# A hybrid attention, state-space and PEER layer: head-by-head decoding, a second buffer for turned tiles, and moved table steps and row copies

## What is computed

```python
h = layer_norm(x)                                   # 512 x 2048
z = h @ w_in                                        # q, k, v, ssm_in and two gates
y_attn = chunk_attention(q, k, v); y_ssm = s5(u)    # 8 heads; 64 groups
y_ssm = y_ssm * sigmoid(y_ssm @ w_ssm_glu)
merged = sigmoid(g_attn) * (y_attn @ w_attn_up) + sigmoid(g_ssm) * (y_ssm @ w_ssm_up)
h = layer_norm(alpha * h + merged @ w_mix_out)
ple = rms_norm(p @ ple_w_in) * sigmoid(h @ ple_w_gate)
# PEER: 8 heads pick 16 of 128 x 128 experts for each token
sc = (h @ w_q) . sub_keys                           # 8 x 2 x 128 scores
cand = top16(sc[0]) + top16(sc[1]);  top_sc, pos = top16(cand)     # pos -> pair of indices
gates = softmax(top_sc)
act = gelu(h . u_table[expert]);  y = sum((gates * act) * v_table[expert])
out = layer_norm(alpha * h + y + ple)
```

## Time and profile before

| | |
|---|---|
| median of 3 runs | 3962.52 us (3962.35 to 3972.41) |
| the profiled execution | 3965.28 us, its span 3963.5 us |
| busy | PE 3700.7 us (93%), DVE 2861.7 (72%), POOL 2312.2 (58%), ACT 1140.4 (29%) |
| mean granted clock of PE | 0.974 of full speed |
| memory traffic | 1020.65 MB read, 344.45 MB written |

### The profile page before, as it was taken

How to read it: one execution, slowest core, us unless ns; L and a number is a source line. 1 busy time by engine, 2 the same in 40 slices (tenths; PEclk the granted TensorE clock), 3 DMA queues, 4 the chain that set the end, 5 groups by cost and what they waited for, 6 DMA issues and landing times. The chain is left out here.

```text
span 3963.5 us, 49639 instructions
## 1 busy us (share of the span) xinstructions
PE 3700.7 (93%) x17969; PEld 3211.3 (81%) x17969; DVE 2861.7 (72%) x3863; ACT 1140.4 (29%) x1377; POOL 2312.2 (58%) x1290
## 2 busy tenths in 40 slices
PE   6999999999988999999999999999918999999998
PEld 5778888787767688879999999999817888888886
DVE  7666666667762445869778656666658999999998
ACT  3232322333211332223333222222202333333332
POOL 7334343344433234446666648888877888887870
PEclk9999999999999999999999999999959999999999
DMA  6888888887877586998998889999878999999994
GB/s 230 279 292 279 291 284 283 288 294 275 296 260 255 185 296 226 387 397 279 351 313 276 276 286 341 339 342 339 330 282 345 388 373 382 383 382 373 386 374 188
DMA packets 409612, 1231.15 MB, mean 311 GB/s; under 512 B 77561, under 2 KB 122633, under 8 KB 327977
## 3 DMA queue, kind: packets, MB, share of 16 engines
q1 hardware_dynamic: 261784, 770.07, 55.9%
q0 software_dynamic: 63488, 302.31, 20.2%
q10 hardware_dynamic: 84240, 157.63, 10.8%
HBM read 1020.65 MB, written 344.45 MB: 344 GB/s over the span
## 5 line engine op out<-in xcount | busy, mean ns | idle before, releaser
L767 POOL TENSOR_TENSOR wlo<-raw,whi 128x1024 fp32r<-128x1024 f32 x296 | 758.8, 2586 | 1075.2 <-ACT whi L1122 527.7
L1315 PE MATMUL bank<-h_hi,whi 128*128 128x384 f32 (+1 forms) x3312 | 1191.9, 360 | 41.6 <-DVE wlo L1642 37.2
L1317 PE MATMUL bank<-h_hi,wlo 128*128 128x384 f32 (+1 forms) x3312 | 1181.3, 357 | 0.0
L1316 PE MATMUL bank<-h_lo,whi 128*128 128x384 f32 (+1 forms) x3312 | 1180.5, 356 | 0.0
L1315 PEld LDWEIGHTS bank<-h_hi,whi 128*128 128x128 f32 x3312 | 625.4, 189 | 99.9 <-DVE wlo L1642 45.4
L1317 PEld LDWEIGHTS bank<-h_hi,wlo 128*128 128x128 f32 x3312 | 624.9, 189 | 50.2
L1316 PEld LDWEIGHTS bank<-h_lo,whi 128*128 128x128 f32 x3312 | 625.6, 189 | 47.9 <-issue 0.2
L1642 DVE TENSOR_TENSOR wlo<-raw,whi 128x2048 fp32r<-128x2048 f32 x240 | 549.3, 2289 | 142.0 <-ACT whi L1241 84.6
L1613 PE MATMUL bank<-whi,ew_hi 128*128 128x512 f32 x1408 | 550.1, 391 | 98.1 <-DVE ew_lo L1642 95.9
L834 POOL DMA_INDIRECT gates_d<-gate_all,place_u x336 | 496.0, 1476 | 148.3 <-issue 129.8
L1615 PE MATMUL bank<-whi,ew_lo 128*128 128x512 f32 x1408 | 548.8, 390 | 0.0
(11 more groups left out here) (302 smaller groups left out, 4713.4 us busy)
## 6 DMA issues: line engine op xcount, KB each, us to landing
raw<-in_weights SPq DMA_DIRECT2D x388, 1024.0 KB
v_rows_d<-in_weights ACTq DMA_DIRECT2D x96, 1024.0 KB
tin<-in_weights SPq DMA_DIRECT2D x162, 512.0 KB, 6.0
u_rows_d<-tout SPq DMA_DIRECT2D x324, 256.0 KB, 6.8
u_rows_d<-u_tout SPq DMA_DIRECT2D x188, 256.0 KB
v_rows_d<-in_weights SPq DMA_DIRECT2D x32, 1024.0 KB
gates_d<-zeros SPq DMA_DIRECT2D x32, 768.0 KB, 16.1
act_d<-act_o ACTq DMA_DIRECT2D x128, 192.0 KB
```

Source lines behind the costliest of these rows:

```text
L767: pool.tensor_tensor(wlo[slot][:, part], raw[slot][:, part], whi[slot][:, part].bitcast(F32), ALU.subtract).then_inc(lo_made, 1)
L1315: pe.matmul(bank, whi[slot][:, cols], rhs_hi(c), start=c == 0, stop=False)
L1316: pe.matmul(bank, whi[slot][:, cols], rhs_lo(c), start=False, stop=False)
L1317: last = pe.matmul(bank, wlo[slot][:, cols], rhs_hi(c), start=False, stop=c == DC - 1)
```

## The change

- `tout` becomes two buffers with a semaphore each. In the heads all steps use the first; from the up stage on they alternate. `u_tout` lies elsewhere, and DVE's up loop is written out.
- `OUT_STEPS` 9, three ahead of each column group; units 4 to 53 are turned in the U stage, 50 of them. In the output stage SP issues `ln_g`, `ln_b` and the ple weights behind slab 12's load and ahead of slab 13's.
- POOL makes the low parts of units 0 and 1 only (`U_POOL` 2), DVE those from 2 on.
- The decoding is cut into four pieces for each of 8 heads, which stand behind the low parts of units 2 to 46 (`decode_slab`); scatters of a head can begin when its `place` is done. `sum_gates` follows `sums_by`.
- Row copies: 24 in the gating stage, one behind each of units 0 to 3, then two in four units up to unit 67.
- Five `u_row` buffers. The dots stand behind units 56 to 122. SP loads V's first weights behind the load of unit 122; DVE makes them behind the low parts of units 124 to 127. The gelu of the dots moves behind ACT's second V slab.

```diff
-U_POOL = 16
+U_POOL, U_TURN = 2, 4
...
-UP_STEPS, OUT_STEPS = 16, 12
+UP_STEPS, OUT_STEPS = 16, 9
...
-U_ROWS = 3
-U_LAYS = SB - HEADS - N_GLU // 2 - (N_Q // 2 - 1) - N_GATE // 2
+U_ROWS = 5
+GATE_LAYS_AT = HEADS + N_GLU // 2 + N_Q // 2 - 1
+U_LAYS_AT = GATE_LAYS_AT + 6
+AUX_FROM = N_U - 6
...
-    return 67 + 4 * k // 7
+    first = TURN_U.stop + 2
+    return first + k * (N_U - 5 - first) // PICKS
+def decode_slab(u):
+    return 2 + u if u < 4 else 6 + (u - 4) * 3 // 2
...
-    tout = sb("tout", [P, 4, DC, 32], c_at + 8 * kb)
+    tout = [sb(f"tout{k}", [P, 4, DC, 32], c_at + at * kb) for k, at in enumerate((8, 24))]
...
+            load_wide(AT_OUT, N_OUT - 4)
+            for k in range(2):
+                sp.wait_ge(tout_stored[k], 64 * TOUTS[k] + 64 * (1 - k))
+            sp.dma_start(ln_g[:, :], row(2)).then_inc(ln1_landed, 16)
+            sp.dma_start(ln_b[:, :], row(3)).then_inc(ln1_landed, 16)
             sp.wait_ge(h_ready, TT)
             sp.dma_start(pw_sb[:, :, :], ple_w).then_inc(ple_landed, 16)
             sp.dma_start(p_sb[:, :, :], p_t).then_inc(ple_landed, 16)
-            for i in range(N_OUT - 4, N_OUT):
+            for i in range(N_OUT - 3, N_OUT):
                 load_wide(AT_OUT, i)
...
+                if e == AUX_FROM:
+                    for t in range(TD):
+                        sp.wait_ge(gate_placed[t], 16 * PICKS)
+                    for h in range(2):
+                        sp.wait_ge(act_stored[h], 16 * 8 + 16)
+                    for q in range(4):
+                        load_aux(0, q)
...
-                dve.wait_ge(tout_stored, 64 * x + 64)
+                if k == 0:
+                    dve.wait_ge(tout_stored[0], 64 * (x if used is None else used) + 64)
+                elif used > 0:
+                    dve.wait_ge(tout_stored[1], 64 * used)
...
-            dve.wait_ge(h_tok_landed, 64)
-            dots, sums = 0, TOPK
+            dots, sums, decoded = 0, TOPK, 0
             for e in range(U_POOL, N_U):
                 if e in TURN_U:
                     turn_unit(e)
                 low_part_of(e - U_POOL, e % 2, raw[e % 2])
-                while sums < min(PICKS, TOPK + 3 * (e - U_POOL + 1)):
+                while decoded < 4 * RH and decode_slab(decoded) <= e:
+                    decode(decoded)
+                    decoded += 1
+                    if decoded == 4 * RH:
+                        tables()
+                while sums < sums_by(e):
                     sum_gates(sums)
                     sums += 1
                 while dots < PICKS and dot_slab(dots) <= e:
...
+                if e >= N_U - 4:
+                    first_weights(e - N_U + 4)
```

More of the change, by code:

```diff
@@ L317, in build_trunk @@
     h_tok = sb("h_tok", [P, D], a_at + 56 * kb)
-    u_row = [w(f"u_row{i}", [P, D], at) for i, at in enumerate((24, 56, 64))]
+    u_row = ([w(f"u_row{i}", [P, D], at) for i, at in enumerate((24, 56, 64))]
+             + [sb(f"u_row{3 + i}", [P, D], c_at + 8 * i * kb) for i in range(2)])
     act_p = w("act_p", [P, PICKS], 75.5)
@@ L1927, in _ @@
                     dve.drain()
-            with dve.Fori(0, DC // 2) as j:
+            for j in range(DC // 2):
                 for s in range(2):
@@ L1958, in _ @@
             for g in range(3):
-                for n in range(4):
-                    turn_slab(HEAD_STEPS + UP_STEPS + 4 * g + n)
+                for n in range(3):
+                    x = HEAD_STEPS + UP_STEPS + 3 * g + n
+                    turn_slab(x, *turned_in(x))
                 dve.wait_ge(blk_done, BLK_OUT + 4 * g + 4)
@@ L2083, in _, with picked @@
             dve.sem_inc(picks_made, 1)
-            dve.tensor_scalar(pos_a[:, :, :], pos[:, :, :], 4, None, ALU.logical_shift_right)
-            dve.tensor_scalar(pos_b[:, :, :], pos[:, :, :], 15, None, ALU.bitwise_and)
-            dve.drain()
-            dve.tensor_copy(pos_af[:, :, :], pos_a[:, :, :])
-            dve.tensor_copy(pos_bf[:, :, :], pos_b[:, :, :])
-            dve.drain()
-            with dve.Fori(0, RH) as j:
-                at, one, two = bass.ds(j * TOPK, TOPK), bass.ds(2 * j, 1), bass.ds(2 * j + 1, 1)
-                wide = [P, TT, TOPK, TOPK]
-                for t in range(TT):
-                    for eq, of in ((eq_a, pos_af), (eq_b, pos_bf)):
-                        tt(eq[:, t, :, :], iota[:, 0:TOPK].unsqueeze(1).to_broadcast([P, TOPK, TOPK]),
-                           of[:, t, at].unsqueeze(2).to_broadcast([P, TOPK, TOPK]), ALU.is_equal)
+            def picked(j):
+                return slice(j * TOPK, (j + 1) * TOPK)
@@ L2098, in _, with keep_index, choose @@
+            def keep_index(j):
                 dve.drain()
-                for eq, half in ((eq_a, one), (eq_b, two)):
-                    tt(eq[:, :, :, :], eq[:, :, :, :], i_all[:, :, half, :].to_broadcast(wide), ALU.mult)
+                for eq, half in ((eq_a, 2 * j), (eq_b, 2 * j + 1)):
+                    tt(eq[:, :, :, :], eq[:, :, :, :], i_all[:, :, half:half + 1, :].to_broadcast(wide), ALU.mult)
+            def choose(j):
                 dve.drain()
                 for eq, sel in ((eq_a, sel_i), (eq_b, sel_j)):
-                    dve.tensor_reduce(sel[:, :, at], eq[:, :, :, :], AX.X, ALU.add)
@@ L2139, in weighted, with decode @@
+            def decode(u):
+                if u % 4 == 0:
+                    compare(u // 4)
+                elif u % 4 == 1:
+                    keep_index(u // 4)
+                elif u % 4 == 2:
+                    choose(u // 4)
+                else:
+                    place(u // 4)
             def weighted(q):
```

217 lines of the change are left out of this document (118 added, 99 removed).

## The result

The change makes the kernel faster, by less than half of what was forecast: 3923.6 us (median of 4 runs, 3920.1 to 3924.3) against 3964.6 (4 runs) for the kernel before; the ratio is 0.9891, 95% interval 0.9875 to 0.9906. That is 41 us less where the prediction says 93 (3869), and it lies just inside the upper end of the range, 3925.

A forecast was written before the change was run, and what follows sets the result against it. Bounds: DVE's store waits in the early stages, then POOL's row of 312 slow indirect DMAs in U. 18 + 18 + 6 + 52 + 2 - 3 = 93 us off gave 3869 us for the median (own range 3835 to 3905, wide 3790 to 3925).

The forecast's parts named there:

- The direction and the place of what bounds: U stage, units 56 to 122: POOL's 312 gathers and scatters hold DVE's dots and so PE; faster, chance 0.92.
- Up stage: Two tout buffers end DVE's wait for the store ahead of up_a: 18 of 22 us won.
- Output stage: Two buffers, nine steps and reordered loads let PE set the pace, the opening gaps staying: 18 of 41 us won.
- Gating stage: Eight of 32 row copies go and PE sets the pace: 6 of 7 us won.
- It fits, nearly ... I let the low part of unit 53 come 446 us after the stage's start.: U stage, units 0 to 55: DVE's load is at most 8.1 us per unit where PE needs 8.32.
- Rival (b): Front of U stays bound by stores: units 4 to 53 at 9.25 us, not 8.4; 42 us, 3911; chance 0.13.
- I take 2.10 ... 665 in all.: U stage: POOL's 312 operations at 2.10 us each, 665 us from first gather to the last dot's end.
- From the last dot to V: End of U: a low part, 2 us, and five units, 42; last dot at 1123, V at about 1169.
- The clock's ramp and the third V slab: Start of V: 2 us won as the clock's ramp after the gap goes, 3 lost loading the third V slab.
- Rival (a): POOL keeps up; DMA traffic bounds units 56 to 122, 570 us for 67 units; about 3780; chance 0.17.
- Rival (c): Up and output stages held by tin and loads, not the store, and POOL takes 2.25 us: 3958; chance 0.04.
- Rival (d): Slower: decode pieces in DVE's queue make units 4 to 46 take 11.3 us each; 125 us, 3994; chance 0.06.

The follow-up runs named there:

- turns_first: h_in_psum with DVE turning the output stage's first two slabs before it adds b_ln_in to res, not after: 3794.4 us.
- three_stores: h_in_psum with h_tok loaded after the last turned unit's store and a third buffer for turned units in the U stage: 3792.2 us.
- dot_one_input: The changed kernel with each dot replaced by a sum of the gathered row alone, one SBUF input (wrong output): 3807.5 us.
- h_in_psum: The changed kernel with h_tok copied once into four idle PSUM banks, where each dot reads its second input: 3812.3 us.
- both: h_in_psum with the edits of turns_first and three_stores together, nothing left out: 3781.0 us.

## Where the prediction held and where it failed

**The direction and the place of what bounds.** Right. PE was held by DVE, DVE by the gathered rows, and those by POOL; with 184 operations fewer the time fell by 112 us. The gap before V went, and PE's loss spread over units 56 to 122, as the text said. The saving was mis-sized all the same: 41 us for 93, because the U stage gave nothing where 52 were forecast. The result is 19 us out of the forecast's own range, 3835 to 3905; in the wide one it lies by 1 us.

**Up stage.** Right and a little low: 23 us gained for 18. DVE does wait for `tin`, 4.8 us in all, but it doesn't reach PE, which is busy all of 174.20 us.

**Output stage.** 14 us for 18. That the opening stays was foreseen, but it was left in the sum as an unavoidable piece. `turns_first` shows that it was an order of two operations in DVE's queue, worth 18 us.

**Gating stage.** 8 us for 6.

**"It fits, nearly ... I let the low part of unit 53 come 446 us after the stage's start."** This is the step that failed first: unit 53 came at +466, 21 us late, with 3 more for a last store that took 16 instead of 12 us. I added up DVE's operations against PE's 8.3 us, and that sum was right (`three_stores` runs at PE's pace with all of them). But a sum of busy times leaves out the loop: transpose, store, free buffer. It goes round once in two units, and the store had become late in busier queues. The row that told it was at hand, 3.59 us of waiting in a kernel with one piece of work less. Rival (b), given 0.13, had the mechanism, with 9.25 us per unit for the 8.8 that were measured: 24 of its 42 us. With the next two misses, 22 and 7 us, and 4 us more than forecast from the early stages, that makes 3918 of the measured 3924.

**"I take 2.10 ... 665 in all."** The second step that failed. The mechanism was right and the size off: 2.15 us per operation, and 687 us from the first gather to the end of the last dot, so 22 us more. The 2.07 of the earlier trace rows comes from the middle of the row; over all of it, less POOL's waits for a buffer, it was 2.04 before. What made it 2.15 no run shows. The "less a little" at the end didn't come, and the way from the last gather to the last dot was taken from the wrong gather (16.8 us instead of 10.6); that it measures 19.3 in after, so that the error did little harm, is luck. The sum took the pace from DVE's busy share ("the busier DVE, the slower POOL"). What counts is DVE's operations with two SBUF inputs, which the prediction names only further down; beside a transpose or a sum of one input there is no stretch. In `dot_one_input` DVE was busier (84%) and POOL faster (1.77 us), so the mix, not the busy share, should have been carried over.

**From the last dot to V:** 53 us for 46, and the prediction's own terms give 44 (1123 + 2 + 42 = 1167, not 1169). The next low part waited 7.6 us for `whi`, and ACT for its slab, while the first weights of V were being loaded.

**The clock's ramp and the third V slab,** 2 us won and 3 lost. V takes 981.5 us to the end of the program, against 979.6. The ramp is gone: before, the first twelve V matmuls start 0.43 us apart, at a granted clock of 0.51, and in after 0.23 from the first on, at 1.00: 2.5 us less. PE's waits for V's low parts rise from 2.1 to 6.2 us instead. Both terms were of the right size.

**Rival (a), POOL keeps up.** It did not, but its price can be read now. With `h_tok` in PSUM the row takes 555 us from the first to the last gather and 578 to the end of the last dot, against the 570 that (a) gave for its 67 units. PE is busy 544.57 of the 555 us and DMA's share is 1.00, at 395 GB/s, so both are full and the runs don't tell which would hold alone. "DMA: Bandwidth & Descriptors" of the Trainium skill, section "Bandwidth", gives about 358 GB/s as a core's part when both cores of the pair stream, and more for one alone. By 358 the 555 us would be 612 (395 x 555 / 358), an estimate; here one core runs, and the figure of the prediction, 3817, applied that part to it.

```profile
2197.00:2752.00 555.00, 544.57 (x3107) 539.27 (x3106) 467.18 (x624) 163.75 (x196) 356.55 (x311) 1.00 1.00 395
```

`h_in_psum` took 32 us more than its 3780: its first gather came at +481.5, where (a) starts its units at +466 (15 us), 578 for 570 are 8, and 50 us instead of 44 from the last dot to V are 6. **Rival (c)** did not occur; priced by its own terms it would be 3952, since it leaves the 6 us of the gating stage alone. **Rival (d)** held nowhere: a unit of the front took 8.8 us, not 10.6.

## What to carry to other kernels

Before you cost a long row of indirect DMAs, look at what DVE reads beside them. If one of its two SBUF inputs can lie in an idle PSUM bank, that is an edit of a few lines; here it was worth 111 us, nearly three times the whole change. When an engine's sum of work just fits, write down the loops through DMA as well (buffer, store, buffer) and divide their length by the number of buffers. And follow each piece of work that a stage drops to where it turns up: the three dropped table steps took back 27 of 37 us.

## What the runs showed of the hardware

An indirect DMA on POOL takes 0.97 us, and 0.30 passes until the next. One that starts under a DVE operation that reads two SBUF operands, whether `TENSOR_TENSOR` or `SCALAR_TENSOR_TENSOR`, is held and ends 0.85 us behind it in the median (191 in the row of after, the longest 3.06 us). Beside a reduction of one operand or an operation with its second operand in PSUM it keeps its 0.97 us, and so it does beside a transpose from SBUF to SBUF (the 41 scatters that lay wholly under one of the transposes in the front of after: 0.96 us on average). `SCALAR_TENSOR_TENSOR` over 128x2048 takes 2.28 us with that operand in PSUM and 2.29 with it in SBUF.

What is still open: in `both`, U takes 1092 us (1704.9 to 2797.1), of which PE is busy 1071. The first gather there still waits for the 200 scatters and not for a store. How many should stand ahead of it, and whether low parts too can be kept from holding POOL, wasn't tried.
